# Moving only the used expert slots through indirect transfers, with a ring of six experts

## What is computed

```python
def hier_moe(x, w_coarse, b_coarse, w_fine, b_fine, w_gate, w_up, w_down):
    xt = x.reshape(B * T, D_MODEL)
    coarse = (xt @ w_coarse) + b_coarse
    g_top, g_idx = lax.top_k(softmax(coarse), 1)               # one of 4 groups
    fine = take(einsum('nd,gde->nge', xt, w_fine) + b_fine, g_idx)
    e_top, e_idx = lax.top_k(softmax(fine), 2)                 # two of its 8 experts
    e_w = e_top / sum(e_top)
    comb = one_hot(g_idx) * (g_top * scatter(e_w, e_idx))      # 32 weights per token, 2 not zero
    h = silu(einsum('nd,edf->nef', xt, w_gate)) * einsum('nd,edf->nef', xt, w_up)
    return einsum('nef,efd->nd', h * comb[:, :, None], w_down)
```

## Time and profile before

| | us |
|---|---|
| median of 3 runs (1708.14 to 1718.1) | 1709.87 |
| the profiled execution | 1702.48 |
| its span, first to last instruction | 1700.8 |

### The profile page before, as it was taken

How to read it: one execution, slowest core, us unless ns; L and a number is a source line. 1 busy time by engine, 2 the same in 40 slices (tenths; PEclk the granted TensorE clock), 3 DMA queues, 4 the chain that set the end, 5 groups by cost and what they waited for, 6 DMA issues and landing times. The chain is left out here.

```text
span 1700.8 us, 16762 instructions
## 1 busy us (share of the span) xinstructions
PE 1243.0 (73%) x6380; PEld 772.4 (45%) x6380; DVE 501.1 (29%) x1014; ACT 332.2 (20%) x572; POOL 189.5 (11%) x221
## 2 busy tenths in 40 slices
PE   1998958947777776189996588888799487666660
PEld 0676634424443333168885345444444344333330
DVE  1288853221111111300002233337722211111114
ACT  1324323110000000200001233337611100000001
POOL 0546520010000000200000100000000100000002
PEclk8799979968888888589999798979999688888885
DMA  6112704169999997332234355420041799999974
GB/s 149 45 50 73 299 6 149 50 240 351 359 361 357 361 367 277 106 87 74 74 106 167 140 196 190 158 99 1 1 148 50 245 368 363 365 358 359 362 253 171
DMA packets 234989, 337.52 MB, mean 198 GB/s; under 512 B 18882, under 2 KB 190914, under 8 KB 234904
## 3 DMA queue, kind: packets, MB, share of 16 engines
q1 hardware_dynamic: 213832, 301.65, 52.1%
q0 software_dynamic: 10112, 34.61, 5.4%
q10 hardware_dynamic: 10976, 0.33, 0.4%
HBM read 295.55 MB, written 41.87 MB: 198 GB/s over the span
## 5 line engine op out<-in xcount | busy, mean ns | idle before, releaser
L650 PE MATMUL psum<-arena 128*64 128x256 f32 x2048 | 288.6, 451 | 146.2 <-DMA arena<-moe_w_up 143.1
L650 PEld LDWEIGHTS psum<-arena 128*64 128x64 f32 x2048 | 175.4, 165 | 271.3 <-DMA arena<-moe_w_up 166.5
L1177 PE MATMUL psum<-arena 128*128 128x272 f32 x768 | 179.3, 397 | 5.9 <-DMA arena<-sb_w_qkv 5.9
L1177 PEld LDWEIGHTS psum<-arena 128*128 128x128 f32 x768 | 147.9, 193 | 37.3 <-issue 6.3
L732 PE MATMUL psum<-arena 128*128 128x512 f32 (+1 forms) x320 | 142.3, 600 | 9.0 <-ACT arena L577 7.9
L969 DVE TENSOR_TENSOR arena<-arena,psum 128x256 f32<-128x256 f32 x32 | 13.5, 421 | 412.7 <-PE psum L650 412.7
L667 PE MATMUL psum<-arena 128*64 128x512 f32 x512 | 116.9, 597 | 19.5 <-DVE arena L973 19.5
L404 PE MATMUL psum<-arena 128*128 128x272 f32 x512 | 121.6, 397 | 9.1 <-ACT arena L467 8.1
L404 PEld LDWEIGHTS psum<-arena 128*128 128x128 f32 x512 | 97.9, 192 | 34.5 <-issue 14.9
L719 POOL DMA_DIRECT2D slots_out<-arena x64 | 34.2, 538 | 607.3 <-DVE arena L979 607.3
L523 DVE SCALAR_TENSOR_TENSOR psum<-arena,vec,psum 128x512 f32<-128x512 f32 x138 | 92.9, 749 | 8.5 <-PE psum L414 8.4
(11 more groups left out here) (228 smaller groups left out, 1262.7 us busy)
## 6 DMA issues: line engine op xcount, KB each, us to landing
arena<-moe_w_gate SPq DMA_DIRECT2D x64, 1024.0 KB, 12.0
arena<-moe_w_up SPq DMA_DIRECT2D x64, 1024.0 KB, 12.3
arena<-moe_w_down SPq DMA_DIRECT2D x64, 1024.0 KB, 12.0
arena<-slots_in SPq DMA_DIRECT2D x64, 256.0 KB, 8.6
slots_out<-arena POOLq DMA_DIRECT2D x64, 256.0 KB, 7.8
arena<-cache_k SPq DMA_DIRECT2D x32, 512.0 KB, 5.7
arena<-cache_v SPq DMA_DIRECT2D x32, 512.0 KB, 5.2
arena<-sb_w_qkv SPq DMA_DIRECT2D x24, 512.0 KB, 3.6
```

The lines of the kernel that those rows point to most:

```text
L650: last = mat(K.ps[m][half[q], 0:FE], xe[:, k, q, :], (wg, wu)[m][u][:, k, :], start=(k == 0), stop=(k == KT - 1))
L1177: last = nc.tensor.matmul(K.ps[2 * u + n][:, 0:HALF], wt[u][:, k, :], HT[:, k, n * HALF:(n + 1) * HALF], start=(k == 0), stop=(k == KT - 1))
```

## The change

The slots of one expert now lie one behind the other (row = expert x 64 + rank; rows past slot 64 go to a region behind all of them). VectorE works out, for every pair, a list of 128 row numbers, one for each partition, in which an unused slot gets a number past the end (`used`). POOL loads a pair's rows with one indirect gather over the 128 partitions and stores its results with one indirect scatter by the same list; numbers past the end fail the bounds check and are dropped without an error. An unused partition of the row buffer keeps whatever the buffer held, and `slots_out` is filled with zeros once, beside `slots_in`. SP no longer loads rows. The weight ring has six experts, three pairs: the third pair lies in memory that routing uses, so SP issues it after routing's last VectorE instruction (`late`). The buffers of the pair loop (`xe`, `yo`, `gs`, `h`, `hT`, two instead of three `xr`) move into the region of the normalised rows, and some regions of the convolution stage move. The path for all rows is changed to the new layout.

The diff, cut to its core:

```diff
-RING = 4
+MAIN = NE * CAP
+FAR = SEQ
+NROWS = MAIN + NE * FAR
+RING = 6
-A_RING = 18976
-A_END = A_RING + RING * EW
+A_END = 44480
+A_RING = A_END - RING * EW
+SLOT0 = (2, 4, 0)
...
-            sp.dma_start(K.xs_dram[0:NE * CAP].rearrange("(n p) c -> p n c", p=P), K.zero_rows.unsqueeze(1).to_broadcast([P, NE * CAP // P, D])).then_inc(K.s_zero, 16)
+            for rows in (K.xs_dram, K.ys_dram):
+                sp.dma_start(rows[0:MAIN].rearrange("(n p) c -> p n c", p=P), K.zero_rows.unsqueeze(1).to_broadcast([P, MAIN // P, D])).then_inc(K.s_zero, 16)
...
             def weights(g):
                 for q in range(2):
-                    load_in(K, sp, layer, 2 * g + q, 2 * (g % 2) + q, K.s_win[g % 2])
+                    load_in(K, sp, layer, 2 * g + q, SLOT0[g % 3] + q, K.s_win[g % 3])
...
-            def rows_in(g):
-                for q in range(2):
-                    sp.dma_start(xr[g % 3][half[q], :], xs_rows[2 * g + q, 0:CAP, :]).then_inc(s_rows[g % 3], 16)
...
             weights(1)
             weights_down(1)
-            sp.wait_ge(s["scattered"], 16 * 2 * NB)
-            for g in range(3):
-                rows_in(g)
-            for g in range(PAIRS - 2):
+            sp.wait_ge(s["late"], 1)
+            weights(2)
+            weights_down(2)
+            for g in range(PAIRS - 3):
                 sp.wait_ge(s["up"], g + 1)
-                weights(g + 2)
-                if g + 3 < PAIRS:
-                    rows_in(g + 3)
+                weights(g + 3)
                 sp.wait_ge(s["out"], g + 1)
-                weights_down(g + 2)
+                weights_down(g + 3)
...
+            def rows_in(g):
+                if g >= 2:
+                    pool.wait_ge(s["turned"], g - 1)
+                pool.indirect_dma_start(xr[g % 2], None, K.xs_dram[0:MAIN], bass.IndirectOffsetOnAxis(ap=K.used[:, g:g + 1], axis=0),
+                                        bounds_check=MAIN - 1, oob_is_err=False).then_inc(s_rows[g % 2], 16)
+
+            pool.wait_ge(s["scattered"], 16 * 2 * NB)
+            pool.wait_ge(s["used"], 1)
+            for g in range(2):
+                rows_in(g)
             for g in range(PAIRS):
+                if g + 2 < PAIRS:
+                    rows_in(g + 2)
                 pool.wait_ge(s["ya"], g + 1)
                 pool.wait_ge(s["yv"], g + 1)
-                for q in range(2):
-                    pool.dma_start(ys_rows[2 * g + q, 0:CAP, :], yo[g % 2][half[q], :]).then_inc(s_store[g % 2], 16)
+                pool.indirect_dma_start(K.ys_dram[0:MAIN], bass.IndirectOffsetOnAxis(ap=K.used[:, g:g + 1], axis=0), yo[g % 2], None,
+                                        bounds_check=MAIN - 1, oob_is_err=False).then_inc(s_store[g % 2], 16)
...
+                v.tensor_scalar(jump[x, b, :], ef[x, b, :], float(FAR - CAP), float(MAIN - CAP), ALU.mult, ALU.add)
...
-                v.scalar_tensor_tensor(out=K.pos[x, b, :], in0=rank[x, b, :], scalar=float(NE), in1=ef[x, b, :], op0=ALU.mult, op1=ALU.add).then_inc(s["pos"], 1)
+                v.scalar_tensor_tensor(out=slot[x, b, :], in0=ef[x, b, :], scalar=float(CAP), in1=rank[x, b, :], op0=ALU.mult, op1=ALU.add)
+                do(v.scalar_tensor_tensor(out=jump[x, b, :], in0=rank[x, b, :], scalar=float(CAP), in1=jump[x, b, :], op0=ALU.is_ge, op1=ALU.mult))
+                do(v.tensor_tensor(slot[x, b, :], slot[x, b, :], jump[x, b, :], ALU.add))
+                v.tensor_copy(K.pos[x, b, :], slot[x, b, :]).then_inc(s["pos"], 1)
...
+            for q in range(2):
+                x = half[q]
+                last = v.tensor_scalar(skip[x, :], K.ps[7][x, NB * NE + q:(NB + 1) * NE:2], within[x, 0:1], float(NROWS), ALU.is_le, ALU.mult)
+            do(last)
+            v.tensor_tensor(K.used[:], skip, K.order[:], ALU.add).then_inc(s["used"], 1)
...
+            dve.sem_inc(s["late"], 1)
```

More of the change, by code:

```diff
@@ L190, in stage_setup @@
     conv_layout(K)
-    rows = K.region(A_END - 2 * D, D)
+    rows = K.conv_rows
     hist = K.region(K.conv_end, 2, D)
@@ L596, in stage_moe @@
              "pos", "scattered", "chain", "wr", "prep", "exp", "gate", "up", "silu", "h", "ht", "hT", "turned", "xe",
-             "out", "ya", "yv")
+             "out", "ya", "yv", "late", "used")
     s = {n: K.sem(L + n) for n in names}
@@ L600, in stage_moe @@
     K.s_wdown = [K.sem(f"{L}wdown{v}") for v in range(RING // 2)]
-    s_rows = [K.sem(f"{L}rows{i}") for i in range(3)]
+    s_rows = [K.sem(f"{L}rows{i}") for i in range(2)]
     s_store = [K.sem(f"{L}store{v}") for v in range(2)]
@@ L633, in stage_moe @@
     gs, h, hT = (K.region(at + i * FE, FE) for i in range(3)); at += 3 * FE
-    xr = [K.region(at + v * D, D) for v in range(3)]; at += 3 * D
-    assert at <= A_PREP
+    xr = [K.region(at + v * D, D) for v in range(2)]; at += 2 * D
+    assert at <= A_RING
     wg, wu, wd = [], [], []
@@ L866, in _ @@
             do(v.memset(brp, NEG))
+            for q in range(2):
+                last = v.tensor_scalar(within[half[q], :], K.order[half[q], 0:1], -float(CAP * q), None, ALU.add)
+            do(last)
             g3 = K.vec[:, :, gain:gain + 1]
@@ L977, in _ @@
                 if g >= 2:
-                    dve.wait_ge(s_store[p], 32 * (g // 2))
+                    dve.wait_ge(s_store[p], 16 * (g // 2))
                 v.tensor_copy(yo[p][:, 512:D], K.ps[5 + 2 * p][:]).then_inc(s["yv"], 1)
-    names = ("in", "turned", "xe", "gate", "up", "silu", "h", "ht", "hT", "y", "ya", "yv", "store", "stored", "w", "zero", "far", "ready", "back", "sum")
+    names = ("in", "turned", "xe", "gate", "up", "silu", "h", "ht", "hT", "y", "ya", "yv", "store", "stored", "w", "zero", "far", "ready", "back", "sum", "hn")
     r = {n: K.sem(f"{L}all_{n}") for n in names}
-    turns = EROWS // P
+    turns = FAR // P
+    again = K.region(A_RING + 2 * EW, NB, D)
     Y = K.region(A_HN, NB, 2, D)
@@ L1027, in _ @@
                 act.sem_inc(r["ya"], 1)
+                for b, rr in enumerate(ROWS):
+                    nc.scalar.activation(again[0:rr, b, :], K.X[0:rr, b, :], ACT.Copy, scale=K.rstd[0:rr, b:b + 1]).then_inc(r["hn"], 1)
                 with act.Fori(0, NE * turns) as n:
```

88 lines of the change are left out of this document (44 added, 44 removed).

## The result

The changed kernel takes 1636.76 us (median; 1634.99 to 1643.03) where the kernel before, beside it, takes 1712.42 (1708.14 to 1718.1): a ratio of 0.956, 95% interval 0.952 to 0.960. The forecast was 1618, range 1597 to 1670. The direction held, and 19 us of the gain are missing. The mean granted TensorE clock is 0.882 (before 0.861).

What follows compares the result with a forecast made beforehand. Transfers were taken to set the expert stages' pace. Per layer -15.9 - 33.3 + 3.5 = -45.7, two layers -91, took the profiled 1702.5 us to 1611; median forecast 1618 us, range 1597 to 1670.

Steps and rivals of the forecast that it cites:

- The rows: Expert stages: moving only used slots by 128-partition lists cuts a pair's row time from 4.3 to 1.92 us, -33.3 us per layer.
- r: Row time per expert pair after the change: 1.92 us, the middle between 1.34 and 2.5.
- the lower bound: Row time per pair if 136 used rows spread evenly over 16 DMA engines: 1.34 us.
- fours: Engines serve partitions in fours, 32 apart: fullest has 93 and 95 rows of 128, about 1.85 us per pair.
- blocks of eight: Each engine serves eight fixed partitions; each half's first block stays full, so dropping relieves nothing: 2.5 us per pair.
- Rows get no cheaper: Rival: dropped slots still moved, or row loads stay slow; only -15.9 + 3.5 a layer left, 1685 us; chance 0.16.
- few engines: Rival: rows left after dropping go to few engines; with two, about 1865 us, slower; chance 0.05.
- The ring: Expert stages: pair 2's weights issued at routing's end, one pair of weights less between the anchors, -15.9 us per layer.
- The cover: Idle DMA before pair 0's up, 17.7 us, into which pair 2's 15.9 us weight load just fits.
- The start: Before pair 0's up: later scatters and a slower first gather, +3.5 us per layer (-0.5 to +4.9).
- At nothing: POOL's gather and scatter issues, SP's dropped row issues, second zero fill and last store: no cost; fill uncovered, 20 us once.
- the term of the weights: Expert pair's 6.29 MB of weights: gate and up 10.9 us at 386 GB/s, down 5.05 at 415, together 15.9 us.

Runs made afterwards that it cites:

- f1: Second run of e1's kernel (changed kernel, weight ring 128 bytes lower), on the same chip as f2: 1613.94 us, 0.940 of before.
- f3: e1's kernel with every slot counted as unused, so no expert rows or results are moved: 1567.22 us, 0.914 of before.
- f2: e1's kernel with each expert's slots dealt over its 64 partitions in another order, run beside f1: 1605.97 us, 0.937 of before.
- e3: Changed kernel with lists that name every slot, so all 128 rows of a pair are moved: 1666.78 us, 0.971 of before.
- e7: e1's kernel with POOL's gather replaced by two plain loads of 64 partitions, scatters still lists: 1665.01 us, 0.973 of before.
- e4: Changed kernel, but weights of pair g+2 issued only after pair g's up and down, memory layout kept: 1670.6 us, 0.972 of before.
- e1: Changed kernel with the whole weight ring moved down by 128 bytes in every partition: 1614.18 us, 0.940 of before.
- e2: Kernel before with its weight ring moved up by 128 bytes in every partition: 1756.48 us, 1.022 of before.

## Where the prediction was right, and the step that left it 19 us off

**The rows, -33.3 per layer: right in size.** With r = 1.92 taken between 1.34 and 2.5, f1 and f3 measure 1.79 and 1.65. The middle was a choice between two bounds for want of knowledge, and that it came out so near is in part luck. The reason given against the lower bound was that an engine with a fixed set of partitions keeps its full share; f2 shows that the partitions matter and that fours are nearer than blocks of eight. Of the 4.3 us per pair 2.5 were saved in layer 0: dropping gave 0.75 of it (e3) and lists over 128 partitions in the place of 64-partition loads about 1.2 (e7). Where the other 0.6 or so come from stays open: no run tried the stores alone, and those of before ran beside down's weights in the slices at 382 to 437 GB/s. "Rows get no cheaper" and "few engines" are out.

**The ring, -15.9 per layer: right.** e4 measures 17.7 and 17.0, off the grid. The cover sufficed: pair 2 is issued at 359.00, and in the 23 us from 365 to 388 DMA is busy 0.97. On the grid it more than suffices. DMA of e1 from 366 to 388 us in forty slices:

```profile
GB/s 387 385 387 384 385 385 387 387 384 412 397 362 419 364 384 382 387 384 387 398 447 398 454 387 454 380 447 387 410 290 253 30 0 0 0 0 0 0 45 117
```

Pair 2 has landed by about 383 us and nothing moves until pair 0's up releases pair 3 at 386.19: some 3 us of the gap are left, so SP does have less than a pair in flight there.

**The start, +3.5 per layer: right in sum.** Pair 0's up ends 5.3 us later than before, 387.94 for 382.68, of which 1.3 were there when pair 1's weights were issued (343.03 against 341.74). The remaining 4.0 (3.6 in layer 1) are 1.1 for the last scatter's issue (0.8 forecast), 0.95 for its landing and 2.0 for the gather; POOL's timeline of after, against the earlier trace rows:

```profile
359.69 0.86 POOL L714 DMA_INDIRECT slots_in<-arena,pos  x1 [0.30 <-issue]
368.52 1.05 POOL L719 DMA_INDIRECT arena<-slots_in,used  x1 [7.97 <-DMA slots_in<-arena,pos]
```

The gather takes 375.19 - 368.52 = 6.7 us where SP's row load took 4.6.

**At nothing: right.** The second fill lands 53.8 us after its issue, at 224, and SP's next issue stands at 235.26 (234.50 before). SP's timeline of after:

```profile
170.21 19.01 SPq L372 DMA_DIRECT2D slots_out<-arena  x1
235.26 0.36 SPq L374 DMA_DIRECT2D conv_state_p<-arena  x1
```

and the row of the list of issues, KB and us to landing:

```profile
slots_out<-arena SPq DMA_DIRECT2D x1, 8192.0 KB, 53.8
```

**The step that failed** is the term of the weights, "6.29 MB a pair", of which gate and up were to take 10.9 us at 386 GB/s and down 5.05 us at 415. Both rates were read from the kernel before and carried over as if they belonged to the transfer. They belong to it at that address. The diff said `A_RING = A_END - RING * EW`, the text on the change listed regions that move, and I did not ask what the new address does. Off the grid gate and up take 4.19 MB / 349 = 12.01 us instead of 10.87, and down 2.10 / 403 = 5.20 instead of 5.08. In the stretch, with 13 pairs, this is 13 x 1.26 = 16 us; measured between after and e1, 13.5 and 13.4. For e2, with 14 pairs, it is 18, and measured 19.0 and 18.5. Why the changed kernel loses 3 us less than the rates say stays open.

e1 puts the ring back, and the sum comes out: a step of 18.1 and 17.6 for 17.8 forecast, 1614 and (f1) 1614 us for 1618. That it comes out so closely is luck in part: by f3 the weights and the dropped rows take 4 us a layer more than forecast for the weights, and by f1 and f3 the moved rows take 2 to 4 less.

## What to carry to other kernels

In this case a rate read from a trace held only for the addresses of that trace. When a change moves a buffer that DMA fills, compare its byte address in the partition, base included, modulo 256 before and after, and look at a load that runs alone to see whether its rate has changed. For lists with unused entries, lay the used ones over the partitions so that no group of them keeps a full share; here dropping 47% of the rows saved 0.75 and 0.92 us a pair where an even spread would have saved 1.2.

## What the runs showed that I had not expected

- Runs of 1 KB per partition that start 64, 128 or 192 bytes off the 256-byte grid load at 348 to 349 GB/s, those on it at 388 to 390; the distance plays no part. Runs of 4 KB lose less, 403 for 413. 128 bytes are worth 23 us to the changed kernel (28 by the ratios) and 37 to the one before (1719.58 to 1756.48 on one chip).
- Rows that the bounds check drops stay in the queue as packets (14208 with 17.87, 35.67 or 51.39 MB), at a cost of 0.2 us per pair at most.
- While loads into 64 partitions are in flight beside weights, DMA moves 203 to 273 GB/s, whether their rows lie together in DRAM or not.
